# First stage of an S5 / gating / convolution block reordered: loads, squares, S5 preparation and transposes

## What is computed

```python
mod = c_silu @ w_ada + b_ada                 # shifts, scales, gains; also for the context
h  = rms_norm(x,  g_mix) * (1 + sc1)  + sh1
hc = rms_norm(xc, g_mix) * (1 + sc1c) + sh1c
u_a, u_ac = (h @ w_in)[:, :512], (hc @ w_in)[:, :512]
z_b = gelu((h @ w_in)[:, 512:1536])          # halves: z_u and v
gate_logits = (h @ w_in)[:, 1536:]
y_a = s5_mixer(u_a, u_ac, ...)               # discretise, two directional scans, readout, GLU
y_b = z_u * (spatial weights applied to layer_norm(v))
x = x + ga1 * ((g_a * (y_a @ w_proj_a) + g_b * (y_b @ w_proj_b)) @ w_out)
x = x + ga2 * conv_ffn(modulate(x))          # w_up, 3x3 depthwise conv, silu gate, w_down
return rms_norm(x, g_final)
```

## Time and profile before

| | us |
|---|---|
| median of 3 runs | 545.24 (541.23 to 546.38) |
| span of the profiled execution | 542.9 |
| PE busy | 499.2 (92%) |
| DVE busy | 319.8 (59%) |
| ACT busy | 103.5 (19%) |
| chain that ended last: PE | 80% |
| of it L611 and L617 (feed-forward) | 41% |

### The profile page before, as it was taken

The page is one execution under the profiler, slowest core; times in us unless marked ns, Lnnn a source line. Parts: engine busy times, 40 slices in busy tenths (PEclk is TensorE's granted clock), DMA queues, the critical chain, the costliest instruction groups (busy, mean ns, idle before and its releaser), DMA issues.

```text
span 542.9 us, 8629 instructions
## 1 busy us (share of the span) xinstructions
PE 499.2 (92%) x3096; PEld 400.2 (74%) x3096; DVE 319.8 (59%) x732; ACT 103.5 (19%) x190; POOL 22.7 (4%) x36
## 2 busy tenths in 40 slices
PE   1799979998489999999999999999999999999993
PEld 0334454897367888888787788888888888888882
DVE  1799989968995001122202499999899999000014
ACT  1422371013311115300011321111111111100010
POOL 2000010000000000000000011111011111000000
PEclk9979999999789999999999999999999999999998
DMA  8980489426996467476679943443334444000002
GB/s 269 421 360 0 156 311 154 155 80 92 212 200 220 145 257 251 173 274 249 226 296 426 406 159 131 164 146 146 138 150 155 155 155 155 0 1 0 1 0 77
DMA packets 23804, 95.87 MB, mean 177 GB/s; under 512 B 6304, under 2 KB 11936, under 8 KB 13152
## 3 DMA queue, kind: packets, MB, share of 16 engines
q1 hardware_dynamic: 17472, 89.14, 46.3%
q10 hardware_dynamic: 5776, 3.97, 5.0%
q0 software_dynamic: 528, 2.36, 1.2%
HBM read 92.87 MB, written 2.59 MB: 176 GB/s over the span
## 4 chain that ended last, share of the span: by engine, by line
PE 80%; DVE 7%; DMA 6%; ACT 3%; ACTq 2%; issue 1%; DVEq 0%; SPq 0%
PE bank L611 27%; PE bank L617 14%; PE bank L464 8%; PE bank L566 5%; PE bank L586 5%; DMA s_region<-k_scratch 3%; PE bank L313 3%; PE bank L343 3%; PE bank L393 3%; PE bank L380 3%; DVE s_region L839 2%; ACTq L736 2%; DMA ctx_region<-ctx_t 2%; PE bank L427 1%; PE bank L302 1%
## 5 line engine op out<-in xcount | busy, mean ns | idle before, releaser
L611 PE MATMUL bank<-h_all,s_region 128*128 128x256 f32 x704 | 152.8, 380 | 0.7 <-ACT ctx_region L807 0.7
L611 PEld LDWEIGHTS bank<-h_all,s_region 128*128 128x128 f32 x704 | 133.0, 190 | 20.2 <-ACT h_all L798 1.2
L1239 DVE SCALAR_TENSOR_TENSOR ctx_region<-ctx_region,pk_sb 128x189 f32<-128x189 f32 (+2 forms) x352 | 127.4, 436 | 0.1
L617 PE MATMUL bank<-ring_region,s_region 128*128 128x256 f32 x352 | 76.5, 379 | 0.0
L617 PEld LDWEIGHTS bank<-ring_region,s_region 128*128 128x128 f32 x352 | 66.9, 190 | 9.1
L464 PE MATMUL bank<-h_all,ring_region 128*128 128x256 f32 x256 | 58.4, 387 | 1.1 <-ACT gates L748 1.1
L464 PEld LDWEIGHTS bank<-h_all,ring_region 128*128 128x128 f32 x256 | 48.8, 193 | 11.7 <-issue 5.2
L1246 DVE SCALAR_TENSOR_TENSOR x_region<-bank,mod,x_region 128x256 f32<-128x256 f32 x8 | 3.5, 480 | 67.5 <-PE bank L617 67.5
L839 DVE TENSOR_TENSOR s_region<-s_region,power 128x2048 f32<-128x2048 f32 (+1 forms) x16 | 38.1, 2420 | 2.1 <-PE bank L366 2.0
L807 ACT ACTIVATE ctx_region<-bank 128x512 f32<-128x512 f32 x22 | 13.1, 597 | 125.9 <-PE bank L611 74.2
L343 PE MATMUL bank<-h_all,ring_region 128*128 128x512 f32 x64 | 32.7, 642 | 4.2 <-ACT h_all L687 4.2
(11 more groups left out here) (155 smaller groups left out, 423.9 us busy)
## 6 DMA issues: line engine op xcount, KB each, us to landing
ring_region<-ring_w SPq DMA_DIRECT2D x41, 1024.0 KB, 6.5
s_region<-up_w SPq DMA_DIRECT2D x33, 1024.0 KB, 4.9
s_region<-early_w SPq DMA_DIRECT2D x4, 1024.0 KB, 24.3
gates<-early_w SPq DMA_DIRECT2D x2, 1024.0 KB, 14.0
s_region<-k_scratch ACTq DMA_DIRECT2D x8, 256.0 KB, 18.4
x_region<-x_t SPq DMA_DIRECT2D x1, 1024.0 KB, 5.2
ctx_region<-ctx_t SPq DMA_DIRECT2D x1, 1024.0 KB, 9.3
s_region<-s5raw SPq DMA_DIRECT2D x2, 512.0 KB, 22.6
```

What stands on the lines that cost most here:

```text
L611: mx = pe.matmul(bank[s % 3][:, half * TOK:(half + 1) * TOK], up_ring[:, s, (half * KD + k) * P:(half * KD + k + 1) * P], h2[:, k, :], sta ...
L617: mx = pe.matmul(bank[4 + m // 2][:, (m % 2) * TOK:(m % 2 + 1) * TOK], up_ring[:, k // 2, (k % 2) * D + m * P:(k % 2) * D + (m + 1) * P], ...
L1239: dve.scalar_tensor_tensor(out=o, in0=a, scalar=cw[:, tile[half], (dy + 1) * 3 + dx + 1], in1=o, op0=ALU.mult, op1=ALU.add).then_inc(s_con ...
```

## The change

1. Loads. `early[1]` goes behind the two w_u units. `log_step` is no longer a load of its own: it is repeated on the host and comes with `a_raw` (96 columns instead of 64). The packed parameters are loaded in two parts, 74 of 554 columns first, the rest (`s_pk2`) at the end of SP's first batch. POOL loads the gating bias after the u matmuls instead of at the start.
2. Squares. They go into `h_all`, even tiles by ACT and odd ones by DVE, x first. PE sums x into bank 6 and context into bank 7, 8 matmuls of 256 columns each; root and reciprocal are taken for x and for context apart. On ACT the order is two Exp, squares of x, Silu, two Sin, root preload, root of x, squares of context, root of context.
3. S5 preparation: `discretise` after k = 0, the powers after k = 1, `b_bar` after k = 2, then the products and sums one step later than before.
4. Transposes: jobs 0 to 7 stand amid the v matmuls, jobs 8 to 15 amid the first z_u unit; z_u goes to banks 2 and 3. The waits of K, of `ca` and of L1031 are as before.

```diff
-            sp.dma_start(early[1], early_w[1]).then_inc(s_early[1], 16)
             for u in (U_INU, U_INU + 1):
                 sp.dma_start(ring[:, u, :], ring_w[u]).then_inc(s_ring[u], 16)
+            sp.dma_start(early[1], early_w[1]).then_inc(s_early[1], 16)
...
+            sp.dma_start(pk_sb[:, PK_EARLY:PKW], pk[:, PK_EARLY:PKW]).then_inc(s_pk2, 16)
...
+            pool.wait_ge(s_unit, U_V)
             pool.dma_start(sgu_b_sb[0:64, :, :], sgu_b[0:1].partition_broadcast(64)).then_inc(s_ln, 16)
             pool.dma_start(sgu_b_sb[64:128, :, :], sgu_b[1:2].partition_broadcast(64)).then_inc(s_ln, 16)
-            pool.wait_ge(s_unit, U_V)
...
-            for k in range(KD):
-                pe.wait_ge(s_sq, 2 * (k + 1))
-                pe.matmul(bank[7][:, :], ones[:, :], squares[:, k % 2, :], start=(k == 0),
-                          stop=(k == KD - 1)).then_inc(s_sq_used, 1)
+            for of, dst, at in ((s_sqx, bank[6], TOK), (s_sqc, bank[7], 0)):
+                for k in range(KD):
+                    pe.wait_ge(of[k % 2], k // 2 + 1)
+                    mx = pe.matmul(dst[:, 0:TOK], ones[:, :], h_all[:, k, at:at + TOK], start=(k == 0), stop=(k == KD - 1))
+                mx.then_inc(s_sq_used, 1)
...
-                if k == 3:
-                    pe.wait_ge(s_std, 1)
+                if k in (2, 3):
+                    pe.wait_ge(s_std, k - 1)
...
+            def transposed_input(job):
+                d, r, q0 = job // 8, (job // 4) % 2, 4 * (job % 4)
+                if job % 4 == 0:
+                    pe.wait_ge(s_wsrc, 2 * d + r + 1)
+                if job >= 2:
+                    pe.wait_ge(s_win, job - 1)
+                for q in range(4):
+                    mx = pe.transpose(bank[4 + job % 2][:, q * P:(q + 1) * P],
+                                      w_src[:, d, r, q0 + q].rearrange("p t h -> p (t h)"), ident[:, :])
+                mx.then_inc(s_tr, 1)
...
+                        if half == 1 and c == 0 and kk == KD // 2 - 1:
+                            mx.then_inc(s_v_ps, 1)
+                        elif c == 1 and kk == KD // 2 - 1:
+                            mx.then_inc(s_unit, 1)
+                        elif kk % 2 == 1:
+                            transposed_input(4 * half + 2 * c + kk // 2)
+                    if half == 1 or c == 1:
+                        transposed_input(4 * half + 2 * c + 1)
...
+                        if i == 0 and k % 2 == 1 and not (mm == 1 and k == KD - 1):
+                            transposed_input(8 + 4 * mm + k // 2)
                 mx.then_inc(s_unit, 1)
+                if i == 0:
+                    transposed_input(15)
...
             pe.wait_ge(s_uchunk, 16 * T)
-            pe.wait_ge(s_uf, KS)
+            pe.wait_ge(s_win, 16)
...
-            act.dma_start(a_raw[:, 0:2 * DP], s5raw[:, 0:2 * DP]).then_inc(s_raw, 16)
-            for g2 in range(2):
-                act.dma_start(a_raw[g2 * N:(g2 + 1) * N, 2 * DP:3 * DP], log_step[g2:g2 + 1].partition_broadcast(N)).then_inc(s_ls, 16)
-            act.dma_start(pk_sb[:, :], pk).then_inc(s_pk, 16)
+            act.dma_start(a_raw[:, :], s5raw[:, 0:3 * DP]).then_inc(s_raw, 16)
+            act.dma_start(pk_sb[:, 0:PK_EARLY], pk[:, 0:PK_EARLY]).then_inc(s_pk, 16)
...
             act.wait_ge(s_ada_ps, KD)
+            transposed_inputs(0)
             for c in range(2):
                 act.wait_ge(*((s_unit, U_V + 2) if c else (s_v_ps, 1)))
                 act.activation(v_tok[:, c, :], bank[6 + c][:, :], ACT.Gelu_apprx_tanh).then_inc(s_v, 1)
+            transposed_inputs(1)
...
             dve.wait_ge(s_pk, 16)
-            dve.wait_ge(s_std, 1)
-            mark(dve.reciprocal(rstd[:, :], rstd[:, :]))
+            for i, at in enumerate((TOK, 0)):
+                dve.wait_ge(s_std, i + 1)
+                mark(dve.reciprocal(rstd[:, at:at + TOK], rstd[:, at:at + TOK]))
             settle()
...
-                if k == 1:
+                if k == 0:
                     discretise()
-                elif k >= 2:
...
+                elif k == 1:
+                    state_powers()
+                elif k == 2:
+                    input_matrix()
+                elif k % 2 == 1:
+                    w_products((k - 3) // 4, (k - 3) // 2 % 2)
+                else:
+                    w_sum((k - 4) // 4, (k - 4) // 2 % 2)
+            w_sum(1, 0)
             w_products(1, 1)
             w_sum(1, 1)
```

More of the change, by code:

```diff
@@ L69, with build @@
 PKW = _at
+PK_EARLY = _PK["pick"][1]
 DP = 2 * PAIRS
-S5RAW = DP * 2 + DP * H * 4
-def build(nc, x_t, ctx_t, pk, s5raw, log_step, early_w, ring_w, up_w, ln, sgu_w, sgu_b, out):
+S5RAW = DP * 3 + DP * H * 4
+def build(nc, x_t, ctx_t, pk, s5raw, early_w, ring_w, up_w, ln, sgu_w, sgu_b, out):
     with ExitStack() as ctx:
@@ L660, in _, with half_of_squares @@
             act.activation(small[:, 2 * DP:3 * DP], small[:, DP:2 * DP], ACT.Exp).then_inc(s_trig, 1)
-            act.wait_ge(s_trig_in, 2)
-            act.activation(small[:, 5 * DP:6 * DP], small[:, 4 * DP:5 * DP], ACT.Sin).then_inc(s_trig, 1)
-            act.activation(small[:, 6 * DP:7 * DP], small[:, 4 * DP:5 * DP], ACT.Sin, scale=0.5).then_inc(s_trig, 1)
+            def half_of_squares(src, at, done):
+                for k in range(0, KD, 2):
+                    act.activation(h_all[:, k, at:at + TOK], src[:, k, :], ACT.Square).then_inc(done, 1)
+            act.wait_ge(s_x, 16)
+            half_of_squares(x_sb, TOK, s_sqx[0])
             act.wait_ge(s_pk, 16)
@@ L669, in _ @@
                            ACT.Silu).then_inc(s_csilu, 1)
+            act.wait_ge(s_trig_in, 2)
+            act.activation(small[:, 5 * DP:6 * DP], small[:, 4 * DP:5 * DP], ACT.Sin).then_inc(s_trig, 1)
+            act.activation(small[:, 6 * DP:7 * DP], small[:, 4 * DP:5 * DP], ACT.Sin, scale=0.5).then_inc(s_trig, 1)
             preload_sqrt()
-            act.wait_ge(s_sq_used, KD)
-            act.activation(rstd[:, :], bank[7][:, :], ACT.Sqrt, scale=1.0 / D, bias=EPS).then_inc(s_std, 1)
+            act.wait_ge(s_sq_used, 1)
+            act.activation(rstd[:, TOK:2 * TOK], bank[6][:, 0:TOK], ACT.Sqrt, scale=1.0 / D, bias=EPS).then_inc(s_std, 1)
+            act.wait_ge(s_ctx, 16)
+            half_of_squares(ctx_sb, 0, s_sqc[0])
+            act.wait_ge(s_sq_used, 2)
+            act.activation(rstd[:, 0:TOK], bank[7][:, 0:TOK], ACT.Sqrt, scale=1.0 / D, bias=EPS).then_inc(s_std, 1)
             def first_rows(k):
@@ L696, in _, with transposed_inputs @@
                 act.dma_start(u_dram[m].rearrange("p t c -> p (t c)"), u_feat[:, m, :, :].rearrange("p t c -> p (t c)")).then_inc(s_u_out, 16)
-            act.wait_ge(s_ada_ps, KD)
[L700 to L707, removed]
+            def transposed_inputs(d):
+                for job in range(8 * d, 8 * d + 8):
+                    act.wait_ge(s_tr, job + 1)
+                    act.activation(w_in_s5[:, d, (job // 4) % 2, 4 * (job % 4):4 * (job % 4) + 4, :].rearrange("p q m -> p (q m)"), bank[4 + job % 2][:, :],
+                                   ACT.Copy).then_inc(s_win, 1)
+            act.wait_ge(s_ada_ps, KD)
+            transposed_inputs(0)
             for c in range(2):
@@ L849, in _, with half_of_squares @@
             t0, t1, t2, t3, k_re, k_im, den, turns = (col(i) for i in range(7, 15))
-            def squares_of_both(k):
-                if k >= 2:
-                    dve.wait_ge(s_sq_used, k - 1)
-                for src, off in ((ctx_sb, 0), (x_sb, TOK)):
-                    dve.tensor_tensor(squares[:, k % 2, off:off + TOK], src[:, k, :], src[:, k, :], ALU.mult).then_inc(s_sq, 1)
-            dve.wait_ge(s_ctx, 16)
-            dve.wait_ge(s_x, 16)
-            for k in range(3):
-                squares_of_both(k)
+            def half_of_squares(src, at, done):
+                for k in range(1, KD, 2):
+                    dve.tensor_tensor(h_all[:, k, at:at + TOK], src[:, k, :], src[:, k, :], ALU.mult).then_inc(done, 1)
             dve.wait_ge(s_raw, 16)
@@ L1161, in _ @@
             dve.wait_ge(s_yb, 4)
+            dve.wait_ge(s_pk2, 16)
             for b in range(2):
```

97 lines of the change are left out of this document (42 added, 55 removed).

## The result

| | before | after |
|---|---|---|
| median, us | 543.62 (541.23 to 546.38, 4 runs) | 551.49 (547.15 to 552.59, 4 runs) |
| span of the profiled execution, us | 542.9 | 550.6 |
| ratio to before | | 1.0113, 95% interval 1.0066 to 1.016 |

Timed once more over 12 runs, the ratio was 1.0109 (1.007 to 1.0147). The kernel is slower by 1.1%, the direction that was forecast, and by about half of the forecast 2.1%. 551.49 lies in the range of 550 to 564.

What follows compares the result with a forecast made beforehand. PE was taken to bound the whole kernel. On the 542.9 us span, K 9.8 later (first stage's -4.9 included) and the clock 1.5 gave 554.2; 2.3 from span to median made 556.5 us, 2.1% slower, range 550 to 564.

Steps and rivals of the forecast that it cites:

- K held by `ca`, the likeliest case: K waits for `ca`, itself behind the last transpose; PE waits some 17 us; 556.5 us, range 551 to 560, chance 0.78.
- The sign of K near 124 to 125: In the new profile K starts near 124 to 125 us; a start before 120 would be wrong.
- the stretch from the end of u to `ca`: Sign in the new profile: from the end of u to the last transpose, near 30 us.
- Part 1: First u tile starts at 24.1 us instead of 28.18, with `early[1]` the last to come; gain 4.1 us (3.1 to 7.1).
- Part 2: The u tiles: waits between tiles go, 0.8 us (0 to 0.8); u ends at 64.0 instead of 68.9.
- Part 3: Transposes at 0.575 us a job, 9.2 for 16; last ends at 93.9, K starts at 124.6, 9.8 us later.
- Part 4: K starts at half clock after its longer pause; price 0 to 2.3 us, taken as 1.5.
- The pay-back at L736: Behind K, waits and clock loss of 12.0 us are all recovered; end at 544.5 us, chance 0.08.
- Unpipelined transposes: Transposes amid other work cost 1.09 us a job; last job at 102, 565 us, chance 0.08.
- transposes that lower the clock: v and z_u run at 1.2 GHz, putting 13.73 + 6.92 us more before the last job; 577 us, chance 0.03.
- The table loads: On ACT in the first stage, a table load and the first activation behind it are 1.29 us apart.
- The rival in which the wait does not arise: K is not held if the last transpose ends before 84.1, so u before 54.2; 530.5 us, chance 0.03.

Runs made afterwards that it cites:

- the undone fourth part: The changed kernel with the 16 transpose jobs again between u and v and z_u back in banks 4 and 5: 535.77 us, ratio 0.9805.
- the fourth part alone: The kernel before with only the transposes moved amid v and z_u: 559.9 us, ratio 1.0247.
- the other order of the passes: The changed kernel with the real `ca` passes first, waiting for 8 and 12 transpose jobs, the imaginary ones behind all 16: 538.99 us, ratio 0.9875.
- The run with the bias: The changed kernel with the two gating bias loads (256 KB) at the start again: one run of 554.62 us.
- The run with `early[1]` forward: The changed kernel with `early[1]` loaded ahead of the two w_u units again: one run of 555.23 us.
- the busy pause: The changed kernel with 39 matmuls without use in PE's pause ahead of K: 556.77 us, ratio 1.021.

## Why the prediction was right in kind and too large

The steps that failed are two terms of the sum: what the first u tile waits for (`early[1]`, where it was the norms), with the stretch behind it, and the price of a transpose job (0.575 us, where it was 0.44). Each put K 1.9 us too late.

**K held by `ca`, the likeliest case: right.** The place, the engine, the wait and its length (17 us forecast, 16.9 measured) are as put, and the undone fourth part, the fourth part alone and the other order of the passes show it as the cause. The slack of 3.45 us, which no view lists as a wait, and the count of what had been put ahead of the last transpose were enough to see it. The sign of K near 124 to 125 was missed (120.89), and the stretch from the end of u to `ca` was 28.1 us, not 30.

**Part 1, the start of the first u tile: the step that named what comes last was wrong.** I held it for `early[1]`, landing at 20.0, and computed `first_rows(1)` at half clock behind it: 24.1. These rows of the changed kernel (DMA from issue to landing; timeline) show 18.3 and the full clock:

```profile
gates<-early_w SPq DMA_DIRECT2D x1, 1024.0 KB, 15.0
...
3.32 0.50 SPq L237 DMA_DIRECT2D gates<-early_w  x1
...
18.28 1.93 PE L319 MATMUL bank<-gates,c_pad 128*32 128x256 f32 x32
...
22.86 3.61 PE L349 MATMUL bank<-h_all,ring_region 128*128 128x512 f32 x4 [1.54 <-ACT h_all L709]
```

Both sets of rows take 1.93 us, 32 instructions. PE came to them from the context's sum, not from idleness. The rows of before had it: there too 32 instructions took 1.93 at this place, and I took my half clock from rows 10 us later. Then the norms were last: the reciprocal ran from 18.80 for 1.76, where I had 18.7 as its end. The term behind that is the context's sum. I let it end 1.3 us behind the last square; PE took 3.7 us for its 16 instructions, and ACT waited 2.9 for them:

```profile
14.17 1.32 ACT L675 ACTIVATE h_all<-ctx_region 128x256 f32<-128x256 f32 x4
14.63 3.72 PE L307 MATMUL bank<-h_all,ones 128*128 128x256 f32 x16 [0.78 <-ACT h_all L675]
...
18.39 0.38 ACT L695 ACTIVATE rstd<-bank 128x256 f32<-128x256 f32 x1 [2.90 <-PE bank L307]
```

The tile started at 22.86, 1.2 us before the forecast 24.1: two misses in opposite directions, `early[1]` too late and the norms too early, so that the miss is small partly by luck. The run with `early[1]` forward confirms that it isn't what the tile waits for. Between the bounds for the landing, 18.3 and 21.0, the lower one was right. The run with the bias points at why: a load of 256 KB there delayed `early[1]` by 2.1 us, so "by bytes" was the wrong price for it. With the shorter stretch of u tiles (39.25 us; I had 39.9) u ended 1.9 us earlier than forecast.

**Part 2: right but for the clock.** The waits between tiles are gone, and the preparation never held PE. The half clock lasted until 26.5, for 3.6 us and not for the 5 that I took as the same in both, which is the likely source of the 0.65 us that the stretch was shorter.

**Part 3, the price of a job: mis-sized.** I took 0.575 us from two jobs in 1.15 us. A job amid matmuls took 0.44, so that 16 took 7.0, and 0.3 was lost once while ACT did its table load and the gelu of v: 7.3 instead of 9.2. The 1.15 was the time of eight instructions from the first start to the last end, and the last one alone is 0.27 long; that tail is covered when a matmul follows. Seven steps from start to start are left: (1.15 - 0.27) / 7 is 0.126, so 0.50 for four. Another pair of the kernel before is closer still, with (1.04 - 0.27) / 7 = 0.11 and the 0.44 that was measured:

```profile
68.90 1.04 PE L366 MATMUL bank<-ident,s_region 128*128 128x128 f32 x8
```

The rows had most of the price; I read them wrongly. I called 0.575 hardly above the lower bound without taking the bound from a row.

These two terms, 1.9 and 1.9, less 0.1 of rounding, are the 3.7 us by which K started ahead of the forecast 124.6.

**Part 4, the clock:** 2.1 where I took 1.5, inside its bounds, and shown by the busy pause.

**The rivals.** The pay-back at L736 did not happen: 0.8 us of the stretch came back, and the readers took 1.0 more. But the stretch is not the fixed one that I summed with either. Unpipelined transposes fall by the 0.44 us a job, and transposes that lower the clock fall too: the granted clock was 1.00 from 60 to 90 us. On this rival the Trainium skill (TensorE: Matmul & The Clock Gate, "Part 4: PE-mode transpose") says that transposes do not count as PE being busy in the same way; no run here shows a stretch of matmuls with transposes in them lose the clock by it. The table loads stayed at 1.29 us to the next activation. The rival in which the wait does not arise was worked out wrongly: behind the end of u, PE needs 43.4 us to K and `ca` needs 60.6, both by the forecast's own terms. The difference of 17 us doesn't hang on when u ends, so no first stage, however fast, takes the wait away; u before 54.2 would only have made K as early as before, and not the kernel 14.7 us faster.

**The size in the end.** Profile against profile, 7.7 us instead of 11.3; by the medians 1.1% instead of 2.1%. At K the forecast was 3.7 us too late, by the two terms above; the clock cost 0.6 more than I took, and 0.6 came back behind K, which I had at nothing. The landing and the clock were inside their bounds, the price of a job was below its lower one. My chance for "within 1%", 0.05, was low for a result of 1.1%.

## What to carry to other kernels

Before work is moved later to fill a gap, list who waits for its last piece, memory reuse included, and how much slack each of them has: here the last transpose moved by 9 us past a slack of 3.45 in front of 30 us of DVE passes. When a consumer overwrites a buffer piece by piece, let each pass wait for its own piece. Price an instruction amid others of its engine by its period in a run, not by the busy time of a short group.

## What the hardware showed that I had not expected

- The sum of squares of x took 5.49 us for 14 instructions, 0.39 each, that of the context 3.73 for 16, 0.23 each, of the same shape, while the windows record a granted clock of 1.00 for both. The first are what PE does first in the program. DVE's last square of x ended at 9.33, so waits for squares explain only the first 1 us. The record seems not to show PE's clock there; that is inferred from the pace alone.
- With a load of 256 KB by POOL at the start, `early[1]` landed 2.1 us later (one run, against a spread of 0.9 us without it).
- PE kept at work through a pause gained 2.1 us at K. Some 64 us behind K's end a pause of 1.65 us was followed by 9 us at a granted clock of 0.50, which cost 5.0.
